# A two-block transformer on one core: the branch projections go from raw float32 products to three split products, and the work around them is re-ordered

## The reference

```
for l in range(DEPTH):                                   # DEPTH = 2
    u = rms_norm(h, norm_mix_pre[l]);  parts = split(u @ w_in[l])
    o_a = diff_attention(...)   # A: 4 heads of 128         o_b = gla(...)         # B: 4 heads of 128
    o_c = mla(...)              # C: 4 heads of 128         o_d = window_gqa(...)  # D: 8 heads of 64
    branches = stack([o_a, o_b, o_c, o_d])               # four of width 512
    gates = sigmoid(gate_logits)                         # four of width 1024, columns of u @ w_in
    merged = sum(einsum('btnw,nwd->btnd', branches, w_branch[l]) * gates, axis=2)
    h = h + rms_norm(merged @ w_out[l], norm_mix_post[l])
    h = h + rms_norm(conv_ffn(rms_norm(h), ...), norm_ffn_post[l])
```

## Time and profile before

| | |
|---|---|
| runs | 2380.94, 2385.72, 2386.41 us |
| profiled execution, its own time | 2385.57 us |
| its span, and mean granted clock | 2383.8 us, 0.972 |
| PE, DVE, ACT, POOL busy | 95%, 61%, 45%, 32% |
| heads, early merge, late merge in layer 0 | 262 to 335, 335 to 365, 365 to 442 us |
| the same in layer 1 | 941 to 1012.5, to 1041, to 1114 us |

### The profile page before, as it was taken

One profiled execution on the slowest core, in us unless ns is written; L12 is line 12 of the kernel. 1 busy time (PEld: TensorE's weight loads), 2 busy tenths in 40 slices (PEclk: granted clock), 3 DMA queues, 4 the chain that ended last, 5 costly groups with the idle time before them and its releaser, 6 DMA issues.

```text
span 2383.8 us, 41243 instructions
## 1 busy us (share of the span) xinstructions
PE 2260.5 (95%) x16564; PEld 2092.4 (88%) x16564; DVE 1460.7 (61%) x2612; ACT 1083.6 (45%) x1996; POOL 771.9 (32%) x727
## 2 busy tenths in 40 slices
PE   7999999899999999999899999999999999888998
PEld 6878679889987778699799899988999999888998
DVE  5865447588777764476798664476644644436543
ACT  5554332455446453413655544424544544445443
POOL 3431102126534631122265244214342242131441
PEclk9999899999999998999999999999999999999999
DMA  7763248546775742477467655644556556533554
GB/s 233 203 189 106 92 164 300 195 141 215 247 238 158 206 141 80 140 278 253 141 216 239 223 172 183 186 133 135 166 186 179 176 186 183 165 126 131 186 180 131
DMA packets 121949, 429.33 MB, mean 180 GB/s; under 512 B 14959, under 2 KB 16927, under 8 KB 121632
## 3 DMA queue, kind: packets, MB, share of 16 engines
q1 hardware_dynamic: 94208, 333.80, 43.3%
q0 software_dynamic: 27408, 91.77, 13.3%
q10 hardware_dynamic: 144, 1.13, 0.1%
HBM read 425.55 MB, written 1.10 MB: 179 GB/s over the span
## 4 chain that ended last, share of the span: by engine, by line
PE 84%; DVE 8%; ACT 5%; issue 2%; POOL 1%; DMA 0%; SPq 0%; DVEq 0%; ACTq 0%
PE bank L386 21%; PE bank L388 20%; PE bank L387 20%; PE bank L751 5%; PE bank L376 3%; PE bank L474 2%; DVE ring_lo L1647 2%; ACT ring_hi L927 1%; PE bank L451 1%; PE bank L466 1%; PE bank L568 1%; DVE u L1635 1%; PE bank L610 1%; PE bank L611 1%; DVE cv_sb L1635 1%
## 5 line engine op out<-in xcount | busy, mean ns | idle before, releaser
L1647 DVE TENSOR_TENSOR ring_lo<-ring,ring_hi 128x1024 fp32r<-128x1024 f32 (+1 forms) x448 | 604.0, 1349 | 516.1 <-ACT ring_hi L927 515.6
L386 PE MATMUL bank<-x_hi,ring_hi 128*128 128x256 f32 (+2 forms) x3008 | 874.9, 291 | 24.7 <-POOL ring_lo L2411 6.0
L387 PE MATMUL bank<-x_lo,ring_hi 128*128 128x256 f32 (+2 forms) x3008 | 864.0, 287 | 0.0
L388 PE MATMUL bank<-x_hi,ring_lo 128*128 128x256 f32 (+2 forms) x3008 | 863.1, 287 | 0.0
L927 ACT ACTIVATE ring_hi<-ring 128x1024 fp32r<-128x1024 f32 (+1 forms) x550 | 566.8, 1034 | 322.9 <-PE bank L388 238.6
L386 PEld LDWEIGHTS bank<-x_hi,ring_hi 128*128 128x128 f32 x3008 | 577.1, 192 | 44.1 <-issue 23.1
L388 PEld LDWEIGHTS bank<-x_hi,ring_lo 128*128 128x128 f32 x3008 | 577.9, 192 | 0.0
L387 PEld LDWEIGHTS bank<-x_lo,ring_hi 128*128 128x128 f32 x3008 | 576.2, 192 | 0.5
L2411 POOL TENSOR_TENSOR ring_lo<-ring,ring_hi 128x1024 fp32r<-128x1024 f32 (+1 forms) x144 | 367.6, 2553 | 590.9 <-ACT ring_hi L927 324.5
L388 PE MATMUL bank<-hid_hi,ring_lo 128*128 128x256 f32 (+1 forms) x1056 | 299.3, 283 | 0.0
L386 PE MATMUL bank<-hid_hi,ring_hi 128*128 128x256 f32 (+1 forms) x1056 | 298.2, 282 | 0.0
(11 more groups left out here) (317 smaller groups left out, 2884.2 us busy)
## 6 DMA issues: line engine op xcount, KB each, us to landing
ring<-in_w_gu SPq DMA_DIRECT2D x192, 512.0 KB, 3.5
ada_ring<-in_ada POOLq DMA_DIRECT2D x144, 512.0 KB, 5.0
ring<-in_w_in SPq DMA_DIRECT2D x136, 512.0 KB, 4.5
ring<-in_ffn_up SPq DMA_DIRECT2D x104, 512.0 KB, 3.5
ring<-in_w_down SPq DMA_DIRECT2D x64, 512.0 KB, 3.5
ring<-in_w_branch SPq DMA_DIRECT2D x32, 512.0 KB, 4.0
ring<-in_ffn_down SPq DMA_DIRECT2D x32, 512.0 KB, 4.8
ring<-in_w_down SPq DMA_DIRECT2D x32, 384.0 KB, 3.3
```

Of the source, the lines that this page charges most:

```text
L386: pe.matmul(b[:, cs], ring_hi[:, i_hi, c0], x1, start=first and k == 0, stop=False)
L387: pe.matmul(b[:, cs], ring_hi[:, i_hi, c0], x2, start=False, stop=False)
L388: m = pe.matmul(b[:, cs], ring_lo[:, i, c0], x1, start=False, stop=last and k == nk - 1)
L1647: dve.tensor_tensor(ring_lo[:, i, 0:cols], ring[:, i, 0:cols], ring_hi[:, n % HIGH, 0:cols].bitcast(f32), ALU.subtract).then_inc(split(n)[ ...
```

## The change

The branch slabs are split like the others, and the 16 branch tiles of a layer too. The high parts of the tiles (`br_hi`) lie in memory that nothing uses any more (the squares, the values, two bias tiles), the low parts (`br_lo`) in the place of `br` itself. ACT makes the high parts: D in head 0, A in head 1, B and C in head 3, the last C tile straight from its bank. DVE makes the low parts: D after head 1, A after head 2, B and C at the start of the merge. PE waits for each of them in the first pair. The copy L1327 goes. The two modulation tiles after each early pair go, and each place of the latent heads has two in place of one (eight tiles per layer moved). The halving L2073 becomes a factor in `z_hi` and `z_lo`.

```diff
-                add(("branch", l, j, s), "w_branch", l * 16 + j * 2 + s, split=False)
+                add(("branch", l, j, s), "w_branch", l * 16 + j * 2 + s)
...
+        sq_r = sb("sq_r", KD, T, dt=f32r)
...
+        br_lo = bx("br_lo", 16, T)
+        bx("up_to_v_t", 4 * T, dt=f32)
+        v_hi = bx("v_hi", 6, T)
+        bx("up_to_bias_sb4", 1648, dt=f32)
+        bias_hi = bx("bias_hi", 2, T)
+        br_hi = [sq_r[:, a, :] for a in (0, 1, 2, 3, 6, 7, 4, 5)]
+        br_hi += [v_hi[:, 4, :], v_hi[:, 5, :], bias_hi[:, 0, :], bias_hi[:, 1, :]] + [v_hi[:, a, :] for a in range(4)]
...
-        ADA = {"head": 2, "mla": 1, "merge": 4, "early": 2}
+        ADA = {"head": 2, "mla": 2, "merge": 4, "early": 0}
```

TensorE, `merge`:

```diff
-                        i, _ = begin(("branch", l, j, s))
-                        if j == 0 and s == 1:
-                            pe.wait_ge(*at(act_, "brc", l))
+                        i, i_hi = begin(("branch", l, j, s))
...
-                                m = pe.matmul(b[:, kept(l)], ring[:, i, (4 * x + k) * P:(4 * x + k + 1) * P], br[:, 4 * (2 * s + x) + k, kept(l)],
-                                              start=k == 0, stop=k == 3)
+                                a, c0 = 8 * s + 4 * x + k, slice((4 * x + k) * P, (4 * x + k + 1) * P)
+                                if j == 0:
+                                    pe.wait_ge(*at(dve_, "br_lo", l, a))
+                                pe.matmul(b[:, cs], ring_hi[:, i_hi, c0], br_hi[a][:, cs], start=k == 0, stop=False)
+                                pe.matmul(b[:, cs], ring_hi[:, i_hi, c0], br_lo[:, a, cs], start=False, stop=False)
+                                m = pe.matmul(b[:, cs], ring_lo[:, i, c0], br_hi[a][:, cs], start=False, stop=k == 3)
```

ScalarE, the new function, its calls in the latent heads ahead of `copy_pt`, and those of head 3 after the second gate and ahead of `out_c`:

```diff
+            def branch_high(l, a, x, *by):
+                act.wait_ge(*at(*by))
+                act.activation(br_hi[a][:, kept(l)], x[:, kept(l)], ACT.Copy).then_inc(*sig(act_, "br_hi", l, a))
...
-                    if hd == 3:
-                        act.wait_ge(*at(act_, "oc", ("C", l, 2)))
-                        act.activation(br[:, 8:11, :], y[:, 4:7, :], ACT.Copy).then_inc(*sig(act_, "brc3", l))
+                    for x in range(4):
+                        if hd == 0:
+                            branch_high(l, 12 + x, br[:, 12 + x, :], act_, "od", ("D", l, x))
+                        elif hd == 1:
+                            branch_high(l, x, br[:, x, :], dve_, "bra", l, x)
...
+                    if hd == 3:
+                        for x in range(4):
+                            branch_high(l, 4 + x, br[:, 4 + x, :], dve_, "brb", l, x // 2, x % 2)
+                        for x in range(3):
+                            branch_high(l, 8 + x, y[:, 4 + x, :], act_, "oc", ("C", l, x))
```

VectorE, the end of a latent head with the new function, the start of `merge`, and its last sum:

```diff
+                    for x in range(4):
+                        if hd == 1:
+                            branch_low(l, 12 + x, br[:, 12 + x, :])
+                        elif hd == 2:
+                            branch_low(l, x, br[:, x, :])
+
+            def branch_low(l, a, x):
+                cs = kept(l)
+                dve.wait_ge(*at(act_, "br_hi", l, a))
+                dve.tensor_tensor(br_lo[:, a, cs], x[:, cs], br_hi[a][:, cs].bitcast(f32), ALU.subtract).then_inc(*sig(dve_, "br_lo", l, a))
...
-                dve.wait_ge(*at(act_, "brc3", l))
+                for x in range(4):
+                    branch_low(l, 4 + x, br[:, 4 + x, :])
+                dve.wait_ge(*at(act_, "br_hi", l, 11))
+                for x in range(3):
+                    branch_low(l, 8 + x, y[:, 4 + x, :])
+                branch_low(l, 11, bank[5])
...
-                    dve.tensor_tensor(tmp[:, 0, cs], tmp[:, 0, cs], tmp[:, 2, cs], ALU.add).then_inc(*sig(dve_, "gated", l, j, "c"))
-                    dve.wait_ge(*at(dve_, "gated", l, j, "c"))
-                    dve.tensor_scalar(y[:, j, cs], tmp[:, 0, cs], 0.5, None, ALU.mult).then_inc(*sig(dve_, "gated", l, j, "y"))
+                    dve.tensor_tensor(y[:, j, cs], tmp[:, 0, cs], tmp[:, 2, cs], ALU.add).then_inc(*sig(dve_, "gated", l, j, "y"))
```

More of the change, by code:

```diff
@@ L172, in build @@
     with ctx:
-        mixer_mem, ffn_mem = ExitStack(), ExitStack()
+        mixer_mem, branch_mem, ffn_mem = ExitStack(), ExitStack(), ExitStack()
         def sb(name, *shape, where=ctx, dt=f32):
@@ L191, in build @@
         y = sb("y", KD, T)
-        sq = sb("sq", KD, T)
+        raw_mem = ExitStack()
+        sq = sb("sq", KD, T, where=raw_mem)
+        raw_mem.close()
+        sq_r = sb("sq_r", KD, T, dt=f32r)
         raw_mem = ExitStack()
@@ L218, in build, with bx @@
         mixer_mem.close()
+        def bx(name, *shape, dt=f32r):
+            return sb(name, *shape, where=branch_mem, dt=dt)
+        br_lo = bx("br_lo", 16, T)
[3 more added lines that the diff above has]
+        bias_hi = bx("bias_hi", 2, T)
+        branch_mem.close()
+        br_hi = [sq_r[:, a, :] for a in (0, 1, 2, 3, 6, 7, 4, 5)]
+        br_hi += [v_hi[:, 4, :], v_hi[:, 5, :], bias_hi[:, 0, :], bias_hi[:, 1, :]] + [v_hi[:, a, :] for a in range(4)]
         def fx(name, *shape, dt=f32r):
@@ L618, in out_c @@
                 pe.wait_ge(*at(act_, "v", un))
-                weighted(un, 0, v_c, slice(0, P), slice(0, P), act_, (act_, "oc", un) if hd < 3 else (act_, "brc", l))
+                weighted(un, 0, v_c, slice(0, P), slice(0, P), act_, (act_, "oc", un) if hd < 3 else (dve_, "br_lo", l, 11))
             def mixers(l):
@@ L737, in merge @@
             def merge(l):
-                for e, *name in ((dve_, "bra", l, 3), (dve_, "brb", l, 1, 1), (act_, "od", ("D", l, 3))):
-                    pe.wait_ge(*at(e, *name))
+                cs = kept(l)
                 for j in range(KD):
@@ L1203, in out_c @@
                 act.wait_ge(*at(pe_, "pv", un, 0))
-                to, name = (y[:, 4 + hd, :], ("oc", un)) if hd < 3 else (br[:, 11, :], ("brc", l))
-                m = act.activation(to, bank[5][:, 0:T], ACT.Copy)
-                m.then_inc(*sig(act_, *name))
+                if hd < 3:
+                    act.activation(y[:, 4 + hd, :], bank[5][:, 0:T], ACT.Copy).then_inc(*sig(act_, "oc", un))
+                else:
+                    act.activation(br_hi[11][:, kept(l)], bank[5][:, kept(l)], ACT.Copy).then_inc(*sig(act_, "br_hi", l, 11))
+            def branch_high(l, a, x, *by):
+                act.wait_ge(*at(*by))
+                act.activation(br_hi[a][:, kept(l)], x[:, kept(l)], ACT.Copy).then_inc(*sig(act_, "br_hi", l, a))
             def mixers(l):
@@ L1349, in merged_high @@
                 act.wait_ge(*at(dve_, "gated", l, k, "y"))
-                act.activation(z_hi[:, k, kept(l)], y[:, k, kept(l)], ACT.Copy).then_inc(*sig(act_, "y_hi", l, k))
+                act.activation(z_hi[:, k, kept(l)], y[:, k, kept(l)], ACT.Copy, scale=0.5).then_inc(*sig(act_, "y_hi", l, k))
             def ffn(l):
@@ L2081, in merged_low @@
                 dve.wait_ge(*at(act_, "y_hi", l, k))
-                dve.tensor_tensor(z_lo[:, k, cs], y[:, k, cs], z_hi[:, k, cs].bitcast(f32), ALU.subtract).then_inc(*sig(dve_, "y_lo", l, k))
+                stt(z_lo[:, k, cs], y[:, k, cs], 0.5, z_hi[:, k, cs].bitcast(f32), ALU.mult, ALU.subtract, "y_lo", l, k)
             def ffn(l):
```

## The result

The changed kernel takes **2362.09 us** (median of 4 runs, 2361.17 to 2365.5) against 2386.06 for the kernel before on the same chip: ratio 0.9905, interval 0.9893 to 0.9918.

What follows compares the result with a forecast made beforehand. The prediction took TensorE, busy for 95% of the span, as the bound. It summed -20.2 + 3.0 + 1.0 - 0.6 = -16.8 us on 2385.57 us to 2369 us, range 2363 to 2378 with rivals.

Steps and rivals of the forecast that it cites:

- Three products for a raw one: Merges of both layers: 32 branch slabs run at the gate slabs' pace on TensorE, -20.2 us.
- The split of the slabs: Merges: copies and subtractions for 32 branch slabs fit beside TensorE's work, 0 us, bounds 0 to 10.
- rival 1: Late merge bound by VectorE with GpSimd's lock, and DMA: late branch slabs give nothing, 2379 us; chance 0.12.
- The branch tiles: Latent heads and merge start: making high and low parts costs 0 us, bounds 0 to 2 a layer.
- Head 3's stall: Latent head 3: added VectorE work delays the normalisation that TensorE's transposes wait for, +1.5 us a layer, +3.0.
- The factor 0.5: Merge chains: the separate halving instruction goes, shortening the last wait of each layer, -0.6 us in all.
- The clock: Head 3: TensorE idling there can lower its granted clock, +1 us in all, bounds 0 and 17.
- 4: Merge: loads come late for slabs used faster, so TensorE waits; at 3 us per late group 2393 us; chance 0.03.
- 2 (cover in head 3): Head 3 has unseen cover, so neither the stall nor its clock loss occurs, 2365 us; chance 0.10.
- 3 (clock low for 17 us in head 3): The clock falls for 17 us in each head 3, 2385 us; chance 0.05.

Runs made afterwards that it cites:

- two_prod: The changed kernel without the product of ring_lo with the high branch parts, one of three per branch slab; 2350.78 us, ratio 0.9853.
- ada_back: The changed kernel with the modulation tiles put back from the latent heads into the early merge; 2374.31 us, ratio 0.9953.
- a_again: The changed kernel run and profiled once more, unedited; 2361.22 us, ratio 0.9904.
- shift_1: The changed kernel with 8 dummy products (1.0 us) ahead of head 3's last gate slab in layer 0 alone; 2363.24 us.
- the 33: 33 runs of the unedited kernel before, taken beside the experiments in three sets, apart from the four runs behind the result.
- out_dve: The changed kernel with the last output tile's low half on VectorE instead of GpSimd, the last sum ahead of the next low half; 2356.14 us.
- h3_first: The changed kernel with head 3's normalisation ahead of the subtraction and tiles, its second tile place moved to the first two early pairs; 2365.09 us.
- h3_again: Second set of runs of the changed kernel with head 3's normalisation first, otherwise unedited; 2360.53 us, ratio 0.9902.
- rest_only: The kernel before with only the moved modulation tiles and the factor 0.5, branch slabs raw; 2381.22 us, ratio 0.9991.

## Why the prediction was right or wrong

- **Three products for a raw one, -20.2: right.** The two stretches that hold the 32 slabs are 10.82 and 10.07 us shorter, and 0.33 of each is the output wait: -20.2.
- **The split of the slabs, 0: right in result, lucky in margin.** PE is 100% busy in the merges. But the argument against rival 1 (idle time of VectorE, slabs split ahead) was weak: two_prod shows VectorE's need at 15.9 to 17.4 us a group against TensorE's 17.18. One more modulation tile (1.14 us) in each late group would be too much by that estimate; it was not run. Eight more in the early merge, in ada_back, made PE wait for 2.8 and 4.5 us.
- **The branch tiles, 0: right.** PE reached the merge's first products without idling; B's low parts (1.49 us) were done 0.85 us before their first reader.
- **Head 3's stall, +3.0: right,** 1.50 + 1.65 = 3.15 us, by the mechanism given. In heads 0 to 2 no new wait came.
- **The factor 0.5, -0.6: right,** 2.65 to 2.32 us in layer 0 and 2.65 to 2.31 in layer 1, -0.67. POOL's lock stayed, as said.
- **The clock, +1.0: this step failed.** I looked for the clock only beside the new stall. There the +1.0 was fair: of five profiles of kernels with the stall, three (a_again, shift_1, two_prod) have one stretch of 3.4 us at 1.2 GHz behind it in layer 1, 1.7 us each, and none has one in layer 0. But three stretches of untouched code became 5.0 us shorter at a higher granted clock, so that the term is about -4: -4.4 +- 1.3 by the split of the runs, 4.1 us by what the times gained outside the marks. My bounds, 0 and 17, left out a gain for no reason that stood in the rows. With -4.4 in its place the sum is -22.2, or 2363.4 us, 1.3 us from the result. What moved it stays open. A smaller share of the miss is the start: the one execution that I subtracted from (2385.57) took 1.9 us more than the mean of the 33.
- **The rivals.** 1 and 4 (merge bound by VectorE, or loads late): refuted, no PE idle time in the merge; but the serial sum behind 1 describes well what VectorE can do at most. 2 (cover in head 3): refuted by the 1.50 us. 3 (clock low for 17 us in head 3): refuted, 3.4 us at most behind the stall.

## What to carry to other kernels

Where TensorE is the bound, price a change of arithmetic by a neighbouring slab of the same form, in the same trace: that term was right to 0.1 us here. VectorE's idle share says little about its margin while GpSimd locks it; add the lock to its sum and compare with the period of a group, and try TensorE's work cut back to see what comes next. This kernel has short idle places all over, and some 60 us of its time are booked to the clock. Edits of a few us moved that part by up to 6 us, down as well as up, so give such a term bounds on both sides. Judge edits of 1 to 5 us by several executions and by the distance between the same two instructions in both traces. Span x clock helps beside them, but it moved by 4.7 us between two profiles of one kernel with the same span.

## What the runs showed of the hardware

- A raw float32 product of 272 columns takes 3.66/8 = 0.457 us, a float32r product 3.027/24 = 0.126 us: 3.63 to 1, so three split products cost 0.83 of a raw one.
- The time booked as lost to the clock (span x (1 - clock)) differs between kernels with nearly the same instructions: 53.6 +- 1.2 us (out_dve) to 63.5 +- 1.1 (h3_first, h3_again). Removing two PE stalls of 1.5 us raised it by 6.0 +- 1.6. Why is open.
- The place of a low clock can be the kernel's own, and not chance: three stretches had 0.95, 0.91, 0.87 in both profiles of the changed kernel and 0.86, 0.86, 0.74 in before and rest_only.
- A subtraction of 1.22 us on VectorE took 3.40 and 3.12 us where GpSimd's (2.53, 2.37) ran beside it: each ended 1.1 us after GpSimd's, so it was blocked for the remaining length, not slowed. In VectorE's busy time the wait is counted as work.
